# Loading the large expert's gate and up blocks by one transfer each instead of two

## The chip, the cores and the metric

The kernel runs on one core of a Trainium2 chip (8 cores, in two dies of four). The metric is device time in microseconds (us) of one launch, the median of several runs. The profile is one further execution, recorded by the hardware profiler. Five engines matter: TensorE (PE; PEld is its weight load), VectorE (DVE), ScalarE (ACT), GpSimd (POOL) and SyncE (SP), which here does nothing but wait and issue transfers. Every transfer is carried by the core's 16 DMA engines.

## What is computed

One decoder layer of 1024 tokens with 1024 columns: an mLSTM mixer, LayerNorm, then a mixture of 32 experts of which every token takes two, and a second LayerNorm. The change touches the experts alone:

```python
def expert_block(args):
    xblk, e = args
    hdn = jax.nn.silu(xblk @ w_gate[e]) * (xblk @ w_up[e])
    return hdn @ w_down[e]
```

The three matrices of an expert (gate 1024x512, up 1024x512, down 512x1024, float32) are 2 MB each, so the 32 experts are 192 MB of weights, and each weight is read once.

## The kernel before

The first 480 us or so hold the mixer, the first LayerNorm and the routing. Then come the experts, sorted by how many tokens they have and worked in sixteen pairs, n = 0 to 15: a large expert (up to 128 rows) and a small one (up to 64 rows). The last 50 us or so weight the experts' rows, add them up, normalise and store.

The large expert's matrices are multiplied in three passes of a faster number type: ACT copies a block into a high part (`hi_large`, line 1000, `whi`), DVE subtracts it to get the low part (`lo_large`, line 1739), and PE multiplies high by high, low by high and high by low (lines 1918 to 1920). Each of the blocks gate, up and down (k = 0, 1, 2) is 128 partitions of 16 KB, and it is handled in halves of 8 KB per partition (p = 0, 1): `halves(p)`. The buffers are single: `raw_b[0]` (named `raw` in the profile) takes the gate block, `raw_b[1]` the up block, `raw_b[2]` the down block. The low part overwrites the raw block in place, so a new block may only be loaded when PE is done with the old low part. The small expert's matrices are used in float32 as they are (lines 2342, 2343, 2360, 2361), from `raw_s`, `raw_up` and `raw_down`, also in halves.

Everything is ordered by hand-written program order on each engine and by semaphores. SP's list for pair i is: the small expert's gate and up halves p = 0 and then p = 1 (line 509, four transfers of 1 MB), the large down block (line 504, two transfers), the small down block (two), and then the next pair's large gate block (two) and large up block (two): twelve transfers of 1 MB. Each waits until PE has gone past the data that it overwrites: the gate halves wait on `g_mm`, which counts the halves of `gate_large`, the up halves on `u2_mm`. The semaphore `ex_landed[k][p]` tells ACT that a half has landed. SP issues the transfers of pairs 0 and 1 and of their blocks with fixed expert numbers; later ones take the number from the sorted list.

ACT's list for pair i (function `pair`) is, in order: the two down halves of `hi_large`; `silu_large`; `hidden_hi`; `hi_large(i + 1, 0, 0)`, the first gate half of the next pair; `silu_small` (line 1032); `xg_hi`; `hi_large(i + 1, 0, 1)`; `y_large`; `hidden_small`; the first up half; `y_large`; the second up half; `y_small`; `x_small`. ACT works this list strictly in order, so a half that hasn't landed holds up all behind it.

PE's list for pair i is: `gate_up_small(i, 0)`, `hidden_large(i)` (line 2311, needs the large silu by way of DVE's `gu_b`), `gate_up_small(i, 1)`, `rows_large(i + 1)` (line 2284), `down_large(i, 0)`, `hidden_small(i)` (line 2351, needs `silu_small` by way of DVE's `gu_s`), `down_large(i, 1)`, `down_small(i)`, `gate_large(i + 1)`, `rows_small(i + 1)` (line 2332), `up_large(i + 1)`. POOL gathers the tokens' rows for each expert and scatters the results to memory, on a queue of its own.

Of the kernel before, what the change touches and what calls it, by code (L numbers as in the profile page):

```python
# [44 lines left out]
FIRST = 2  # L45
# [26 lines left out]
def halves(p):  # L72

    return slice(p * HALF, (p + 1) * HALF)


def build(nc, x_rows, x_cols, meta_cols, w_in, b_gates, head_norm_w, w_out, ln1_g, ln1_b, w_group, b_group, w_router,
# [144 lines left out]
    def over(t, name, shape, dt=F32):  # L222
        return nc.alloc_sbuf_tensor_at(name, list(shape), dt, offset=offsets[t])
# [20 lines left out]
    raw_b = [raw[1], over("wlo1", "raw_b1", [P, PIECE]), over("wlo2", "raw_b2", [P, PIECE])]  # L244
# [109 lines left out]
    def sem(name):  # L354
        if name not in S:
            S[name] = nc.alloc_semaphore(name)
        return S[name]
# [3 lines left out]
    ex_landed = [[sem(f"ex_landed{k}_{p}") for p in range(2)] for k in range(3)]  # L361
# [25 lines left out]
    N = {n: sem(n) for n in names}  # L387

    gate_w = w_gate.rearrange("e (p k) n -> e p (k n)", k=KC)
    up_w = w_up.rearrange("e (p k) n -> e p (k n)", k=KC)  # L390
# [40 lines left out]
    def _(sp):  # L431
# [55 lines left out]
        def half_of(src, e, p):  # L487
            if isinstance(e, int):
                return src[e, :, halves(p)]
            return src[bass.ds(e, 1), :, halves(p)].rearrange("e p n -> p (e n)")  # L490
# [3 lines left out]
                sp.dma_start(raw_b[k][:, halves(p)], half_of((gate_w, up_w, down_w)[k], e, p)).then_inc(ex_landed[k][p], 16)  # L494

        def load_large(n, e, k):
            for p in range(2):
                if k == 0:
                    sp.wait_ge(N["g_mm"], n * 2 + (p - 1))
                elif k == 1:  # L500
                    sp.wait_ge(N["u2_mm"], n * 2 + (p - 1))
                else:
                    sp.wait_ge(N["y2_mm"], n * 3 + (p - 1))
                sp.dma_start(raw_b[k][:, halves(p)], half_of((gate_w, up_w, down_w)[k], e, p)).then_inc(ex_landed[k][p], 16)
# [57 lines left out]
        def load_next_large(i):  # L562
            if isinstance(i, int) and i + 1 < FIRST:
                large = i * 2 + 2
            else:
                if isinstance(i, int) and i + 1 == FIRST:
                    sp.wait_ge(N["ordered"], 1)
                large = expert_at(i * 2 + 2)
            load_large(i + 1, large, 0)
            load_large(i + 1, large, 1)  # L570

        def load_pair(i, ahead=1):
            fixed = isinstance(i, int) and i < FIRST
            small = i * 2 + 1 if fixed else expert_at(i * 2 + 1)
            for p in range(2):
                for k in range(2):
                    load_small(i, small, k, p)
            load_large(i, i * 2 if fixed else expert_at(i * 2), 2)
            for p in range(2):
                load_small(i, small, 2, p)  # L580
            if ahead:
                load_next_large(i)
# [245 lines left out]
    def _(act):  # L828
# [167 lines left out]
        def hi_large(n, k, p):  # L996
            if isinstance(n, int) and n == 0 and k == 2:
                act.wait_ge(N["y_mm"], 2 * NT)
            act.wait_ge(ex_landed[k][p], n * 16 + 16)
            a.activation(whi[k][:, halves(p)], raw_b[k][:, halves(p)], ACT.Copy).then_inc(e_hi[k], 1)  # L1000

        def xg_hi(n):
# [48 lines left out]
        for p in range(2):  # L1051
            hi_large(0, 0, p)
# [4 lines left out]
        act.wait_ge(N["h1_done"], NT + 1)  # L1057
        act.dma_start(h1_dram[T - P:T, :], z1[1][:]).then_inc(h1_stored[1], 16)
        hi_large(0, 1, 0)
        xg_hi(0)  # L1060
        hi_large(0, 1, 1)
        act.wait_ge(N["w_arg"], 1)
        a.activation(r_g4[:], r_g4[:], ACT.Exp)
# [1403 lines left out]
```

## Time and profile before

| | us |
|---|---|
| median of 3 runs | 1074.08 |
| lowest and highest | 1072.32, 1075.74 |
| the profiled execution | 1074.68 |
| its span | 1073.0 |

Busy shares of the span: PE 95%, PEld 68%, DVE 53%, ACT 40%, POOL 16%. The mean granted clock of PE is 0.987 of full speed. The program moves 288.17 MB in 71465 packets, 45812 of them under 8 KB. PE's busy time is modelled from pipelined matmuls and isn't a measure of how near it is to its peak. "DMA share" is the mean busy share of the 16 DMA engines; it can read slightly over 1 because a packet's bytes and time are booked at its end.

### The profile page before, as it was taken

The page shows a single profiled execution, that of the slowest core. Times are in us where ns is not written, and L with a number is a line of the kernel's source. Part 1 is how long each engine was busy: PE and PEld are TensorE (multiplying, and loading weights), DVE is VectorE, ACT ScalarE, POOL GpSimd, SP SyncE. Part 2 cuts the span into 40 slices and gives each one's busy share as a digit, 9 for nine tenths or more (in the row PEclk, how much of TensorE's full clock was granted, in tenths as well). Part 3 has the DMA queues.
Part 4 walks back from the last instruction along what each step waited for, and adds up shares of the span by engine and source line. Part 5 has one row for each costly group of instructions (what it writes and reads, how often), then busy time and mean ns, then how long its engine had stood idle before and what let it go on. Part 6 is the DMA issues. An engine that isn't in the chain of part 4 may idle for free.

```text
span 1073.0 us, 14469 instructions
## 1 busy us (share of the span) xinstructions
PE 1019.5 (95%) x5051; PEld 733.5 (68%) x5051; DVE 565.7 (53%) x1040; ACT 434.0 (40%) x574; POOL 173.7 (16%) x208
## 2 busy tenths in 40 slices
PE   8999999999999999999999989989998989989993
PEld 7878999778888788866665556646564556645541
DVE  4320503135465787878556645454445535465488
ACT  5322213223435410024555535454455535555452
POOL 3101111100000000012232212302332113430200
PEclk9999999999999999999999999989999999999997
DMA  8613314541211543456999999999999999999893
GB/s 301 242 47 121 123 44 133 172 146 40 80 42 60 196 157 138 177 203 220 400 418 414 413 412 404 383 386 403 415 401 374 415 402 387 419 385 406 349 359 157
DMA packets 71465, 288.17 MB, mean 269 GB/s; under 512 B 14352, under 2 KB 22680, under 8 KB 45812
## 3 DMA queue, kind: packets, MB, share of 16 engines
q1 hardware_dynamic: 60336, 258.35, 62.0%
q0 software_dynamic: 9920, 24.94, 6.1%
q10 hardware_dynamic: 1156, 4.20, 1.0%
q8 instruction: 32, 0.52, 0.2%
q14 instruction: 21, 0.17, 0.1%
HBM read 262.47 MB, written 33.56 MB: 276 GB/s over the span
## 4 chain that ended last, share of the span: by engine, by line
PE 66%; DMA 19%; DVE 6%; issue 4%; ACT 3%; DVEq 2%; POOL 0%; SPq 0%; POOLq 0%; ACTq 0%
PE bank L1918 15%; DMA raw_b<-l_w_down 14%; PE bank L1920 14%; PE bank L1919 14%; PE bank L2342 6%; DMA raw<-l_w_gate 5%; PE bank L2360 2%; ACT whi L1000 2%; PE bank L2103 1%; PE bank L2105 1%; PE bank L2284 1%; PE bank L2108 1%; PE bank L2152 1%; PE bank L2351 1%; PE bank L2311 1%
## 5 line engine op out<-in xcount | busy, mean ns | idle before, releaser
L1739 DVE TENSOR_TENSOR wlo<-raw_b,whi 128x2048 fp32r<-128x2048 f32 x64 | 146.0, 2289 | 171.8 <-ACT whi L1000 170.7
L1000 ACT ACTIVATE whi<-raw_b 128x2048 fp32r<-128x2048 f32 x64 | 122.1, 1912 | 47.8 <-DMA raw_b<-l_w_down 47.4
L2342 PE MATMUL bank<-raw_up,xT_s 128*64 128x512 f32 x256 | 123.7, 628 | 0.0
L2343 PE MATMUL bank<-raw_s,xT_s 128*64 128x512 f32 x256 | 123.7, 628 | 0.0
L1918 PE MATMUL bank<-whi,x_blocks 128*128 128x512 f32 x288 | 115.5, 401 | 0.9 <-ACT num L947 0.6
L1920 PE MATMUL bank<-whi,x_blocks 128*128 128x512 f32 x288 | 112.4, 390 | 0.0
L1919 PE MATMUL bank<-wlo,x_blocks 128*128 128x512 f32 x288 | 112.3, 390 | 0.0
L1918 PE MATMUL bank<-whi,xghi 128*128 128x512 f32 x256 | 103.4, 404 | 0.0
L1920 PE MATMUL bank<-whi,xglo 128*128 128x512 f32 x256 | 99.7, 389 | 0.0
L1739 DVE TENSOR_TENSOR lo_b<-raw,whi 128x2048 fp32r<-128x2048 f32 x32 | 73.2, 2287 | 42.8 <-ACT whi L1000 41.8
L2342 PEld LDWEIGHTS bank<-raw_up,xT_s 128*64 128x64 f32 x256 | 34.0, 143 | 67.9 <-issue 66.1
L1000 ACT ACTIVATE whi<-raw 128x2048 fp32r<-128x2048 f32 x32 | 61.1, 1913 | 24.1 <-DMA raw<-l_w_gate 19.5
L1918 PEld LDWEIGHTS bank<-whi,xghi 128*128 128x128 f32 x256 | 48.0, 188 | 22.7 <-issue 12.4
L1918 PEld LDWEIGHTS bank<-whi,x_blocks 128*128 128x128 f32 x288 | 54.1, 188 | 12.2 <-issue 1.8
L1920 PEld LDWEIGHTS bank<-whi,x_blocks 128*128 128x128 f32 x288 | 54.1, 188 | 11.7
L1919 PEld LDWEIGHTS bank<-wlo,x_blocks 128*128 128x128 f32 x288 | 54.2, 188 | 10.0
L1183 DVE TENSOR_TENSOR wlo<-raw,whi 128x2048 fp32r<-128x2048 f32 x10 | 22.5, 2288 | 69.5 <-ACT whi L834 69.5
L2360 PE MATMUL bank<-raw_down,hT_s 128*64 128x512 f32 x128 | 58.4, 598 | 0.0
L2361 PE MATMUL bank<-raw_down,hT_s 128*64 128x512 f32 x128 | 58.4, 598 | 0.0
L1920 PEld LDWEIGHTS bank<-whi,xglo 128*128 128x128 f32 x256 | 48.1, 188 | 10.4
L1918 PE MATMUL bank<-whi,ghi 128*128 128x512 f32 x128 | 53.6, 419 | 0.0
L1919 PE MATMUL bank<-wlo,ghi 128*128 128x512 f32 x128 | 50.1, 392 | 0.0
(425 smaller groups left out, 2017.7 us busy)
## 6 DMA issues: line engine op xcount, KB each, us to landing
raw<-l_w_gate SPq DMA_DIRECT2D x32, 1024.0 KB, 17.3
raw_b<-l_w_down SPq DMA_DIRECT2D x32, 1024.0 KB
raw_up<-l_w_up SPq DMA_DIRECT2D x32, 1024.0 KB
raw_down<-l_w_down SPq DMA_DIRECT2D x32, 1024.0 KB
raw_s<-l_w_gate SPq DMA_DIRECT2D x32, 1024.0 KB
raw_b<-l_w_up SPq DMA_DIRECT2D x32, 1024.0 KB, 15.8
raw<-l_w_in SPq DMA_DIRECT2D x5, 2048.0 KB, 9.5
yy<-expert_rows SPq DMA_DIRECT2D x8, 1024.0 KB, 8.6
```

Source lines behind the costliest of these rows:

```text
L1000: a.activation(whi[k][:, halves(p)], raw_b[k][:, halves(p)], ACT.Copy).then_inc(e_hi[k], 1)
L1183: tt(wlo[g % 2][:, c], raw[g % 2][:, c], whi[g % 2][:, c].bitcast(F32), ALU.subtract).then_inc(N["lo_done"], 1)
L1739: tt(lo_b[k][:, halves(p)], raw_b[k][:, halves(p)], whi[k][:, halves(p)].bitcast(F32), ALU.subtract).then_inc(e_lo[k], 1)
L1918: t.matmul(out, lh, rh, start=first, stop=False)
L1919: t.matmul(out, lh, rl, start=False, stop=False)
L1920: return t.matmul(out, ll, rh, start=False, stop=last)
L2103: t.matmul(ps[N_BANK[h % 2]][:, 0:DV + 1], ew[:, h, :], vext[c % 2][:, h, :], start=True, stop=False)
L2105: t.matmul(ps[N_BANK[h % 2]][:, 0:DV + 1], qsT[:, h, :], cst[:, h, :], start=False, stop=True).then_inc(N["n_mm"], 1)
L2342: t.matmul(ps[7][0:SMALL, :], xT_s[:, kk, :], wu[:, kk, :], start=kk == 0, stop=kk == KC - 1)
L2343: last = t.matmul(ps[7][SMALL:, :], xT_s[:, kk, :], wg[:, kk, :], start=kk == 0, stop=kk == KC - 1)
L2360: t.matmul(ps[7][0:SMALL, :], hT_s[:, k, :], wd[:, k, 0:512], start=k == 0, stop=k == FC - 1)
L2361: last = t.matmul(ps[7][SMALL:, :], hT_s[:, k, :], wd[:, k, 512:], start=k == 0, stop=k == FC - 1)
```

## The change

From n = 2 on, the gate block and the up block of the large expert are each loaded by one transfer of 128 rows of 16 KB. It waits until both halves of the old block have been used, and it signals `ex_landed[k][0]` alone. Both halves of `hi_large` wait for that one semaphore. The down block, all small blocks, and pairs 0 and 1 stay as they are.

```diff
         def load_large(n, e, k):
+            if k < 2 and not (isinstance(n, int) and n < FIRST):
+                sp.wait_ge((N["g_mm"], N["u2_mm"])[k], n * 2)
+                whole = (gate_w, up_w)[k]
+                sp.dma_start(raw_b[k][:], whole[e] if isinstance(e, int) else whole[bass.ds(e, 1)].rearrange("e p n -> p (e n)")).then_inc(ex_landed[k][0], 16)
+                return
             for p in range(2):
                 if k == 0:
                     sp.wait_ge(N["g_mm"], n * 2 + (p - 1))
@@
         def hi_large(n, k, p):
             if isinstance(n, int) and n == 0 and k == 2:
                 act.wait_ge(N["y_mm"], 2 * NT)
-            act.wait_ge(ex_landed[k][p], n * 16 + 16)
+            halves_land = k == 2 or (isinstance(n, int) and n < FIRST)
+            act.wait_ge(ex_landed[k][p if halves_land else 0], n * 16 + 16)
             a.activation(whi[k][:, halves(p)], raw_b[k][:, halves(p)], ACT.Copy).then_inc(e_hi[k], 1)
```

## Rows read from the trace of the kernel before

**Rows 1.** The page's 40 slices: DMA busy tenths, and what they moved.

```profile
DMA  8613314541211543456999999999999999999893
GB/s 301 242 47 121 123 44 133 172 146 40 80 42 60 196 157 138 177 203 220 400 418 414 413 412 404 383 386 403 415 401 374 415 402 387 419 385 406 349 359 157
```

**Rows 2.** Windows: busy us (instructions) by engine, PE clock, DMA share, GB/s.

```profile
571.00:595.00 24.00, 24.00 (x114) 15.94 (x111) 12.34 (x13) 13.32 (x14) 6.97 (x8) 1.00 1.01 425
605.00:1000.00 395.00, 368.66 (x1693) 226.32 (x1690) 198.55 (x138) 200.56 (x199) 102.09 (x92) 0.98 1.00 400
712.00:724.00 12.00, 12.00 (x58) 7.11 (x56) 8.80 (x6) 8.31 (x10) 1.83 (x4) 0.96 0.91 361
636.00:642.00 6.00, 5.50 (x20) 2.02 (x20) 2.99 (x4) 2.51 (x2) 0.00 (x0) 0.72 1.01 426
```

**Rows 3.** The chain that ended last, 580 to 1010: start, us, what.

```profile
587.84 17.26 DMA raw<-l_w_gate
605.13 1.92 ACT whi L1000
...
613.89 17.69 DMA raw_b<-l_w_down
...
991.91 15.29 DMA raw_b<-l_w_down
```

**Rows 4.** DMA packets of 12:20, 571:595 and 605:1000, and gate issues in 605:1000.

```profile
DMA packets 1369, 3.28 MB, mean 411 GB/s; under 512 B 49, under 2 KB 56, under 8 KB 1369
...
DMA packets 1606, 10.21 MB, mean 425 GB/s; under 512 B 219, under 2 KB 219, under 8 KB 503
...
DMA packets 25040, 157.87 MB, mean 400 GB/s; under 512 B 4332, under 2 KB 4332, under 8 KB 7222
...
raw<-l_w_gate SPq DMA_DIRECT2D x22, 1024.0 KB, 18.0
```

**Rows 5.** SP's timeline, gate and up issues in pairs 3 and 6.

```profile
620.43 3.05 SPq L504 DMA_DIRECT2D raw<-l_w_gate  x2
626.98 3.05 SPq L504 DMA_DIRECT2D raw_b<-l_w_up  x2
...
728.81 3.05 SPq L504 DMA_DIRECT2D raw<-l_w_gate  x2
```

**Rows 6.** Who waited for whom in the whole trace: us in total, times, longest.

```profile
ACT whi L1000 <- DMA raw_b<-l_w_down: 47.4, 26, 4.7
...
PE bank L2311 <- DVE gu_b L1761: 25.2, 12, 5.2
...
ACT whi L1000 <- DMA raw<-l_w_gate: 19.5, 13, 3.1
```

**Rows 7.** ACT's timeline in pairs 3 and 14: gate halves and small silu.

```profile
605.13 1.91 ACT L1000 ACTIVATE whi<-raw 128x2048 fp32r<-128x2048 f32 x1 [2.60 <-DMA raw<-l_w_gate]
607.06 0.60 ACT L1032 ACTIVATE sg_s<-bank 64x512 f32<-64x512 f32 x1
...
608.65 1.91 ACT L1000 ACTIVATE whi<-raw 128x2048 fp32r<-128x2048 f32 x1
...
984.59 0.60 ACT L1032 ACTIVATE sg_s<-bank 64x512 f32<-64x512 f32 x1
```

**Rows 8.** PE's timeline: small and large hidden transposes of pairs 3, 5 and 14 (the large ones of the pair after).

```profile
610.10 0.66 PE L2351 MATMUL bank<-ident,gu_s 64*128 64x64 f32 x4 [0.76 <-DVE gu_s L1770]
...
636.50 0.75 PE L2311 MATMUL bank<-ident,gu_b 128*128 128x128 f32 x4 [3.24 <-DVE gu_b L1761]
...
678.97 0.66 PE L2351 MATMUL bank<-ident,gu_s 64*128 64x64 f32 x4 [1.34 <-DVE gu_s L1770]
...
708.12 1.12 PE L2311 MATMUL bank<-ident,gu_b 128*128 128x128 f32 x4 [5.23 <-DVE gu_b L1761]
...
988.09 0.69 PE L2351 MATMUL bank<-ident,gu_s 64*128 64x64 f32 x4
...
1012.12 0.75 PE L2311 MATMUL bank<-ident,gu_b 128*128 128x128 f32 x4 [0.84 <-DVE gu_b L1761]
```

## The prediction

> **What bounds the kernel now.** I read the page's slices first. From about 510 us to 1000 us the DMA engines are busy nine tenths or more in every slice and move some 400 GB/s [rows 1]. That is the expert stage. The windows say it closer: a share of 1.00 to 1.01 throughout, 425 GB/s in a good stretch, 400 GB/s as the mean of 605:1000 [rows 2]. PE is busy 368.66 us of those 395, so it idles too, and the chain shows why: it runs through a gate load of 17.26 us and a down load of 17.69 us, each time followed by ACT's copy, and in between there is only PE work [rows 3]. A gate half takes 18.0 us from issue to landing [rows 4], although 1 MB (1.05e6 bytes) at 425 GB/s needs only 2.47 us. So some 15 us of other transfers stand before it in the queue. The stage is bound by how fast the queue drains; when a transfer is issued hardly matters as long as the queue stays filled. What the reader should keep in mind is where this bound touches the engines: ACT waits for landings, 47.4 us for down and 19.5 us for gate [rows 6], and since ACT works in order, PE then waits 25.2 us ahead of line 2311 for a silu that stood behind the down copies. These waits are the slack with which PE pays for being faster than the queue.
>
> **The change part by part.**
>
> *Packets.* Pairs 2 to 15 have two merged blocks each: 28 blocks, 28 transfers fewer. A half is 128 rows of 8 KB on 16 engines, that is 8 packets an engine, and one very small packet an engine tells that it has ended (the packets under 512 B). So each block saves 8 row packets and 1 end packet per engine, 28 x 9 = 252. The price of a packet comes from two full stretches. In 12:20 there are 1369 packets of 2.4 KB, 16 x 8 us / 1369 = 93.5 ns each; in 571:595 there are 1606 of 6.4 KB, 16 x 24 us / 1606 = 239.1 ns each [rows 4]. The straight line through both is 5.4 ns a packet and 0.0368 ns a byte (435 GB/s without packets). The saving is 252 x 5.4 ns = 1.4 us. No row shows a 16 KB packet, so the bounds are wide. At one end nothing is saved, if a row is cut into the old packets anyway. At the other end: by the same line the 157.87 MB and 25040 packets of 605:1000 should take (25040 x 5.4 ns + 157.87e6 x 0.0368 ns) / 16 = 371 us, and they take 395. These 24 us are slow packets and thin queues. Gate and up have 22 issues each there, 44 x 1.05 = 46 of the 157.87 MB, 29%; if long rows freed them of all of it, that would be 7 us more, 8.4 in all. I take 1.4: the line is drawn through measured stretches, and 571:595 is nearest in kind, 8 KB rows in a full queue; nothing in the rows ties the 24 us to the length of rows.
>
> The Trainium skill (DMA: Bandwidth & Descriptors, Anatomy of one DMA, and Bandwidth) gives a transfer about 2.0 us fixed and bytes/436e3 us, and wants transfers of 1 MiB and more. By it each merged block would save 2.0 us, 56 us for the 28, if transfers followed each other one by one; the rows of 571:595 show the opposite, 425 GB/s with 1 MB transfers, so that fixed part already lies beside others' data.
>
> *Issue.* The first half is no longer issued when half the old block is used but with the second. In SP's rows the two issues of a block span 3.05 us and the single one takes some 0.35, so the first goes out 2.7 us later [rows 5]. The second goes out when it did. Behind it on SP stand the up block, which waits for a later PE event anyway, and the next small blocks, which also do. With 15 us of queue ahead, 2.7 us are hidden. The cover is thinnest after a long stall: in 712:724 the share is 0.91 and the rate 361 GB/s [rows 2], and the gate issue comes at 728.81, right behind the pair's large and small down blocks, 4 transfers that alone take 9.9 us. If the cover were gone, each such place would cost up to 2.7 us. I take zero.
>
> *Landing.* Now the first gate half is seen only when the whole block has landed. That is later by the second half's transfer: at least 2.47 us, and under 3.5 us, as in pair 3 the second copy starts at 608.65 without a wait, 3.5 us after the first [rows 7]. ACT is waiting for exactly this half in 13 pairs (2 to 14), and behind it stands the small silu. In pair 3 the silu moves from 607.06 to 609.5. From the silu to the small transposes (line 2351) it is 3.04 us (607.06 to 610.10), and PE already stood 0.76 us there; so PE loses 2.5 us, likewise in pair 5 [rows 8]. In pair 14 the silu at 984.59 becomes 987.1, the transposes 990.1 instead of 988.09: 2.0 us. The same working for all thirteen pairs gives 0 to 2.5 us each and 20 us together. It is not added to the time, since the next thing PE waits for is the down block, which comes out of the queue when it did: PE idles 3.24 us at 636.50 and 5.23 us at 708.12 [rows 8], and such idle sums to 25.2 us over 12 pairs [rows 6]. A loss of 2.5 there is paid out of an idle of 2 to 5. The last pair is the exception: its idle is 0.84 us against a loss of 2.0, so 1.2 us come through: the last down block's landing ends the stage, and no later idle pays for them. The up block is harmless: its copies stand later in ACT's list, where second halves are taken without a wait, and PE uses them 10 us later.
>
> The Trainium skill (same page, Why a DMA increments its semaphore by 16 and not by 1) says that only the full count tells that data has landed, and an intermediate one not which bytes. That speaks against the change: ACT can't start on the first 8 KB of a row that is there. The rows agree in so far as ACT's copies begin only at landings.
>
> *ACT's second wait* on the same semaphore passes at once: nothing. *POOL's* gathers and scatters share the engines with longer packets and may land a few us later; they are asked for some 20 us ahead, so nothing.
>
> *Sum*, against the profiled 1074.68: -1.4 + 1.2 = -0.2, so 1074.5; against the median of 1074.08 it is 1073.9. The profiled execution is 0.6 above the median and inside the span of the three runs.
>
> **Rivals.**
>
> *Faster: long rows raise the rate.* The queue is the bound, so each per cent of rate counts in full. For it: 400 GB/s as the mean against 425 in a good stretch. Against it: 8 KB rows already reach 425 of the 435 that the line gives. Price between 1.4 and 8.4 us, middle 5: 1069. Chance 0.21.
>
> *Slower: the stall moves to line 2351 and takes the clock down.* Three pairs, of which 3 and 5 are shown, would have an idle of over 3.1 us there (0.76 + 2.5 in pair 3, 1.34 + 2.5 in pair 5) [rows 8]. After the idle of 3.24 us at 636.50 the granted clock was 0.72 over 636:642 [rows 2], between 1.2 and 2.4 GHz, so 6 x 0.28 = 1.7 us of work were lost. It decides from where loss and slow clock together (2.5 + 1.7) exceed the idle ahead of line 2311, which is about 3 us in most pairs; then the small blocks are released later and the queue gets as thin as in 712:724. Three such places with 1.7 us and 1.2 at the end make 6.3 us, with no gain from packets: 1080.4. Against it: the idle ahead of line 2311 shrinks by what is lost before, so there the clock stays up. Chance 0.21.
>
> *The change does nothing to packets*: rows are cut as before. Then only the 1.2 us are left: 1075.3. Chance 0.06. My forecast has 0.52.
>
> **How the numbers follow.** About 0.3%, 3.2 us, is what a measurement of this kernel can tell from no change. The forecast and the last rival lie within it: 0.58. Faster by more 0.21, slower by more 0.21. The range reaches into both outer cases, down to 1068.5 (just past the middle of the faster one) and up to 1079.5 (just short of the slower one's 1080.4), leaving out some 0.2.
>
> **What would show it.** Right: 252 x 16 = 4032 packets fewer; SP's gate issue as one, at the time of the old second; ACT's wait for gate longer by some 2.5 us in each of 13 pairs and PE's wait ahead of line 2351 up from near nothing to 15 to 20 us; PE's wait ahead of line 2311 down by about as much; the last down block landed some 1 us earlier than 1007.2 (991.91 + 15.29) [rows 3]. Wrong: a rate of 605:1000 clearly over 400 GB/s (the faster rival), or a share below 0.97 and more stretches of half clock (the slower one). The sum also fails if the down block lands later than it did, for then PE's idle is no cover.

## The result, and the profile after

| | before | changed |
|---|---|---|
| median of 22 runs each, us | 1073.97 | 1078.15 |
| lowest and highest | 1072.23, 1084.05 | 1075.30, 1084.08 |
| ratio, 95% interval | | 1.0035 (1.0022 to 1.0048) |
| span of the profiled execution | 1073.0 | 1077.6 |
| mean granted clock of PE | 0.987 | 0.978 |

The changed kernel is slower by some 4 us, where no change was forecast (1073.9 us, within the 0.3% that a measurement can tell). The line numbers move: 1000 becomes 1006, 1032 becomes 1038, 2311 becomes 2317, 2351 becomes 2357.

4032 packets fewer for the same bytes, and a rate over the stage that isn't higher. First the page's line of packets, then the stage as a window (busy us of each engine, granted clock, DMA share, GB/s), then its packets:

```profile
DMA packets 67433, 288.17 MB, mean 267 GB/s; under 512 B 13904, under 2 KB 22232, under 8 KB 45364
```

```profile
605.00:1000.00 395.00, 373.20 (x1696) 230.56 (x1694) 196.71 (x144) 197.40 (x198) 92.60 (x91) 0.97 1.00 399
```

```profile
DMA packets 21633, 157.75 MB, mean 399 GB/s; under 512 B 3946, under 2 KB 3946, under 8 KB 6816
```

Against [rows 2, 4] that is 399 GB/s beside 400, with a share of 1.00 in both. Then who waited for whom (total us, times, longest), to be laid beside [rows 6]:

```profile
ACT whi L1006 <- DMA raw<-l_w_gate: 48.8, 14, 5.2
...
PE bank L2357 <- DVE gu_s L1776: 24.6, 13, 3.5
...
ACT whi L1006 <- DMA raw_b<-l_w_down: 5.5, 8, 0.9
...
PE bank L2317 <- DVE gu_b L1767: 0.5, 1, 0.5
```

Ahead of the small transposes PE had waited for this in the kernel before:

```profile
PE bank L2351 <- DVE gu_s L1770: 2.8, 3, 1.3
```

ACT's wait has changed places: from down (47.4 us, now 5.5) to gate (19.5, now 48.8). PE's wait went with it: 25.2 us ahead of the large hidden transposes have become 0.5, and 2.8 us ahead of the small ones have become 24.6. In sum nothing was added (28.0 us before, 25.1 now). The queue stays full as before, and PE just stands in another place.

The end of the stage differs. First the chain of waits (start, us, what), then ACT's and PE's timeline of pairs 14 and 15:

```profile
974.83 13.75 DMA raw<-l_w_gate
...
992.75 0.68 DVE gu_s L1776
```

```profile
988.60 1.91 ACT L1006 ACTIVATE whi<-raw 128x2048 fp32r<-128x2048 f32 x1 [2.27 <-DMA raw<-l_w_gate]
...
1008.01 3.71 ACT L1006 ACTIVATE whi<-raw_b 128x2048 fp32r<-128x2048 f32 x2
```

```profile
993.57 0.66 PE L2357 MATMUL bank<-ident,gu_s 64*128 64x64 f32 x4 [0.52 <-DVE gu_s L1776]
...
1016.66 0.75 PE L2317 MATMUL bank<-ident,gu_b 128*128 128x128 f32 x4
```

The first gate copy of pair 15 in the kernel before was this:

```profile
982.65 1.91 ACT L1000 ACTIVATE whi<-raw 128x2048 fp32r<-128x2048 f32 x1 [1.23 <-DMA raw<-l_w_gate]
```

Before, the last DMA step in the chain was the last down block [rows 3], and PE stood 0.84 us for it at 1012.12 [rows 8]. Now it is the last gate block, n = 15. Its landing at 988.60 starts ACT's copy, and from there the chain goes through ACT, DVE and PE with no further transfer. Both down copies run back to back at 1008.01 without a wait, and PE comes to its transposes at 1016.66 without one. The profiled execution of the changed kernel was already 1.9 us late before the first merged transfer (its large transposes of pair 0 start at 508.76, before 506.88). Of the 4.5 us at the last large transposes (1016.66 - 1012.12) 2.6 us are therefore the stage's, and the tail behind adds nothing.

One thing in these two profiles doesn't come from the last landing. PE's large transposes of pair 14 stand ahead of it, and they are late already (before, then changed):

```profile
979.96 0.75 PE L2311 MATMUL bank<-ident,gu_b 128*128 128x128 f32 x4 [2.15 <-DVE gu_b L1761]
```

```profile
984.86 0.75 PE L2317 MATMUL bank<-ident,gu_b 128*128 128x128 f32 x4
```

That is 4.9 us, 3.0 without the late start. SP issues the last gate block late, too, since the issue waits for PE: at 974.83, where the second half went out at 967.7 before (the pair of issues starts at 964.98, the second some 2.7 us on). Less the 1.9 us of late start this is 5.2 us.

```profile
964.98 3.05 SPq L504 DMA_DIRECT2D raw<-l_w_gate  x2
```

### The profile page after: what moved, and what is told of

Its sections match the earlier page's. It is cut to its first block, busy times and chain, and to the rows that moved or that the text cites. A ratio compares the mean times of both kernels' runs of the same rounds, so it can differ in the third digit from the quotient of the medians.

```text
span 1077.6 us, 14399 instructions
## 1 busy us (share of the span) xinstructions
PE 1027.1 (95%) x5051; PEld 741.4 (69%) x5051; DVE 564.0 (52%) x1040; ACT 430.8 (40%) x574; POOL 171.6 (16%) x208
## 4 chain that ended last, share of the span: by engine, by line
PE 66%; DMA 19%; DVE 6%; issue 4%; ACT 3%; DVEq 2%; SPq 0%; ACTq 0%
DMA raw<-l_w_gate 18%; PE bank L1924 16%; PE bank L1926 15%; PE bank L1925 15%; PE bank L2366 5%; ACT whi L1006 2%; PE bank L2348 2%; PE bank L2109 1%; PE bank L2111 1%; PE bank L2114 1%; PE bank L2357 1%; PE bank L2158 1%; DVE gu_s L1776 1%; PE bank L2427 1%; PE bank L2431 1%
## 5 line engine op out<-in xcount | busy, mean ns | idle before, releaser
L2348 PE MATMUL bank<-raw_up,xT_s 128*64 128x512 f32 x256 | 116.7, 599 | 0.0
L2349 PE MATMUL bank<-raw_s,xT_s 128*64 128x512 f32 x256 | 116.7, 598 | 0.0
L1006 ACT ACTIVATE whi<-raw 128x2048 fp32r<-128x2048 f32 x32 | 61.1, 1913 | 53.4 <-DMA raw<-l_w_gate 48.8
L1924 PE MATMUL bank<-whi,ghi 128*128 128x512 f32 x128 | 59.0, 461 | 0.0
L1925 PE MATMUL bank<-wlo,ghi 128*128 128x512 f32 x128 | 55.3, 432 | 0.0
```

Source lines behind the costliest of these rows:

```text
L1924: t.matmul(out, lh, rh, start=first, stop=False)
L1925: t.matmul(out, lh, rl, start=False, stop=False)
L2348: t.matmul(ps[7][0:SMALL, :], xT_s[:, kk, :], wu[:, kk, :], start=kk == 0, stop=kk == KC - 1)
L2349: last = t.matmul(ps[7][SMALL:, :], xT_s[:, kk, :], wg[:, kk, :], start=kk == 0, stop=kk == KC - 1)
```

## The experiments

All times are against the kernel before on the same chip; 0.3% is 3.2 us. "Held" says that ACT's first gate copy waits for the whole block ahead of the small silu.

| kernel | gate transfer | held | ratio (95%) |
|---|---|---|---|
| changed | merged | all pairs | 1.0035 (1.0022 to 1.0048) |
| changed, again | merged | all pairs | 1.0043 (1.0022 to 1.0065) |
| only gate merged | merged | all pairs | 1.0046 (1.0030 to 1.0061) |
| only up merged | halves | no | 1.0007 (0.9992 to 1.0021) |
| late issue | halves | no | 0.9995 (0.9981 to 1.0010) |
| late look | halves | all pairs | 1.0018 (1.0004 to 1.0032) |
| both late | halves | all pairs | 1.0027 (1.0007 to 1.0047) |
| both late, gate only | halves | all pairs | 1.0013 (0.9991 to 1.0035) |
| changed, small silu first | merged | no | 1.0013 (0.9987 to 1.0038) |
| the same, again | merged | no | 0.9990 (0.9968 to 1.0012) |
| before, small silu first | halves | no | 0.9999 (0.9979 to 1.0019) |
| changed, PE kept busy | merged | all pairs | 1.0044 (1.0021 to 1.0067) |
| changed but the last gate | merged, last in halves | all but the last | 1.0022 (1.0004 to 1.0040) |
| only the last gate merged | halves, last merged | last | 1.0041 (1.0020 to 1.0062) |
| last pair written out (control) | halves | no | 0.9987 (0.9966 to 1.0008) |
| the control, last pair held | halves | last | 1.0021 (0.9996 to 1.0047) |
| first three merged | merged for n = 2, 3, 4 | those | 1.0001 (0.9981 to 1.0021) |

### Issue, look or transfer

The change does three things: it issues the first half later, it looks at it later, and it makes rows of 16 KB. Each could be the cause, and the expectations name them by letters. Theory A is the late look: ACT holds the small silu until the whole gate block is there. Theory B is the late issue of the first half. Theory C is that rows of 16 KB are slow in the queue. The first runs take one each. Late issue (in `load_large`):

```diff
-                    sp.wait_ge(N["g_mm"], n * 2 + (p - 1))
+                    sp.wait_ge(N["g_mm"], n * 2 + (0 if late else p - 1))
```

(the same for `u2_mm`; `late` is true from n = 2 on)

> From the third pair on, the first halves of gate and up are issued only when PE has used both halves of the old block, 2.7 us later than before; rows stay 8 KB and ACT looks at each half by itself. Theory A expects nothing, within 1 us of before, as some 15 us of queue stand ahead of the transfer. Theory B expects the loss here: +3 to +4 us. Theory C expects nothing.

Ratio 0.9995: the late issue by itself costs nothing that can be measured (at most 1 us by its interval). Theory B falls as a cause by itself.

Late look (in `hi_large`):

```diff
+            if k < 2 and p == 0 and not (isinstance(n, int) and n < FIRST):
+                act.wait_ge(ex_landed[k][1], n * 16 + 16)
             act.wait_ge(ex_landed[k][p], n * 16 + 16)
```

> From the third pair on, gate and up stay two transfers of 8 KB rows, issued when they always were, but ACT's first copy of each block waits for both halves. Theory A (the late look: ACT, which works in order, holds the small silu until the whole gate block is there, and PE stands at the small hidden transposes) expects most of the change's loss: +3 to +4 us against before, the waiting of PE moved from the large to the small hidden transposes. Theory B (the late issue of the first half) expects no loss, within 1 us of before. Theory C (16 KB rows are slow in the queue) expects no loss either.

Ratio 1.0018, +1.9 us. Its waits have the changed kernel's pattern without any merged transfer:

```profile
ACT whi L1002 <- DMA raw<-l_w_gate: 47.3, 14, 5.3
...
PE bank L2353 <- DVE gu_s L1772: 24.1, 13, 3.5
...
ACT whi L1002 <- DMA raw_b<-l_w_down: 7.1, 11, 1.2
```

So the moved waits are the late look's doing, as theory A says, but only about half of the loss came with them (0.4 to 3.4 us by the interval).

One block each:

```diff
-            if k < 2 and not (isinstance(n, int) and n < FIRST):
+            if k == 0 and not (isinstance(n, int) and n < FIRST):
```

(`k == 1` for up, and `halves_land` to match)

> Only the gate block is merged into one transfer of 16 KB rows, up stays in halves. Theory A expects the whole loss, +3 to +5 us, since only the gate copy stands ahead of the small silu. Theory C expects half of the loss, +2 us. Theory B expects at least half, too.

> Only the up block is merged into one transfer of 16 KB rows, gate stays in halves. Theory A expects no loss, and if fewer packets are worth something a gain of up to 0.7 us (half of the forecast 1.4): -0.7 to 0. Theory C expects the other half of the loss, +2 us. Theory B expects +2 us.

1.0046 and 1.0007: the loss is in gate, and none is seen in up (its interval ends at +2.3 us). Half of the long rows are thus free of loss, and free of gain too. Both late edits together, for both blocks and for gate alone, keep 8 KB rows and give the rest of the change:

> Everything of the change but the merged transfer: from the third pair on the two gate halves and the two up halves go out together, at the time of the second, as 8 KB rows, and ACT looks only when both are there. The late look alone gave a ratio of 1.0018, the gate merged alone 1.0046. If the rest of the loss is in the 16 KB rows (theory C), this gives +1.5 to +2.5 us against before, like the late look alone. If late issue and late look add up to more than each alone (theory A with B), it gives the change's whole +4.

> Only gate, as two transfers of 8 KB rows that go out together at the time of the second, and ACT looks when both are there: the counterpart of the run with only gate merged (1.0046). If the merged transfer itself costs (16 KB rows land later than two transfers of 8 KB rows), this gives +1.5 to +3 us against before; if not, +4 to +5.

1.0027 and 1.0013. The three held kernels with halves give +1.4 to +2.9 us, the three merged ones +3.8 to +4.9. The changed kernel, repeated beside the first of them:

> The changed kernel once more, on the chip of its neighbours: +3 to +5 us against before by every theory. Its trace should again have its waits at gate (45 to 50 us) and a last gate landing 4 us later than that of the first half before.

### Taking the silu out from behind the gate copy

```diff
         def pair(i):
             ...
-            hi_large(i + 1, 0, 0)
             silu_small(i)
             xg_hi(i + 1)
+            hi_large(i + 1, 0, 0)
             hi_large(i + 1, 0, 1)
```

(this is ACT's list; and on DVE `lo_large(i + 1, 0, 0)` behind `times_up_small(i)` and `xg_lo(i + 1)`)

> The changed kernel, but ACT does the small silu and the rows' high part before the first gate copy, and DVE the small product and the rows' low part before the first gate subtraction. Theory A (a copy that waits for the gate block holds up the small silu) expects the wait of PE at the small hidden transposes to vanish and the loss with it: within 1 us of before or faster. If the loss is in the queue (theory C), some +2 us stay.

> The changed kernel with the small silu ahead of the first gate copy, a second time (1.0013 with a wide interval the first time). If the held-up silu is the whole cause: within 1 us of before, both results together at 1.000 to 1.001. If the merged transfers cost by themselves: +2 us.

> The kernel before with the same reordering of ACT and DVE. Theory A expects it near before, 0 to -1 us: PE's waits at the small transposes sum to only 2.8 us there, and its wait for the down block stays. If it is faster by more, the order was costing more than its visible waits.

With the merged transfers as they are, 1.0013 and 0.9990: taken together the loss is gone, and no gain is seen. The first of them alone has an interval up to 4.1 us and would not show it. On its chip its median is 1075.96 us, against 1079.49 for the changed kernel. The kernel before doesn't care (0.9999). The waits of the first (PE at the large transposes for `gu_b`, ACT at down) are back where they were:

```profile
ACT whi L1006 <- DMA raw_b<-l_w_down: 48.0, 25, 4.0
...
PE bank L2317 <- DVE gu_b L1767: 25.7, 11, 4.4
```

So theory C falls as a cause by itself: the same packets cost nothing that is seen here once ACT no longer holds the silu for them.

### The clock

In the changed kernel the longest idle at the small transposes is 3.49 us (PE's timeline), and a window behind it has a granted clock of 0.50, the 1.2 GHz level:

```profile
651.42 0.71 PE L2357 MATMUL bank<-ident,gu_s 64*128 64x64 f32 x4 [3.49 <-DVE gu_s L1776]
```

```profile
651.00:657.00 6.00, 5.58 (x16) 4.35 (x16) 6.00 (x6) 3.44 (x4) 0.00 (x0) 0.50 0.97 385
```

The mean clock of the run is 0.978. Eight small matmuls ahead of the wait keep PE at work:

```diff
-        def hidden_small(s):
+        def hidden_small(s, ends=False):
+            if not ends and not (isinstance(s, int) and s < 2):
+                awake(4, 8)
             pe.wait_ge(N["gu_s_done"], s + 1)
```

(`ends` is true for the last pair alone.)

> The changed kernel, but from the third pair to the last but one PE does eight small matmuls on a constant (some 1.1 us at full clock, their result is overwritten) ahead of its wait for the small hidden product, in time that it idles. Theory F (part of the loss is the granted clock, which falls to the lower level after an idle at the small hidden transposes) expects the clock of the run back at 0.983 or more and 1 to 3 us of the loss gone, so +1 to +3 us against before. Without F it stays at +3.5 to +4.5, or is worse by what the matmuls cost.

The clock came back, to 1.00 over the stage, and the time did not:

```profile
605.00:1000.00 395.00, 382.78 (x1879) 246.44 (x1878) 197.78 (x140) 198.90 (x199) 84.37 (x91) 1.00 1.00 399
```

Ratio 1.0044, with an interval from 2.3 to 7.2 us: nothing of the loss is seen to come back. The falling clock accompanies the loss and isn't its main cause; a share of up to some 1.5 us (3.8 - 2.3) isn't excluded. While the queue sets the period, PE's speed is free. Behind the last gate block it isn't: in "both late, gate only" the granted clock was 0.58 over 990:993 and 0.85 over 993:996, behind the small transposes of pair 14, and there the end came 90.9 us after the start of the last gate copy, 2.0 us more than in the other kernels that hold it (below).

### One-off or pair by pair

If the queue absorbs the stall in every pair but the last (theory D), merging in the last pair alone must cost as much as in all, and merging in the first ones nothing. If the loss builds up pair by pair (theory E), one merged pair must cost next to nothing. For the first the pass i = last - 1 of SP's and ACT's pair loops is written out behind the loop:

```diff
-        with sp.Fori(4, last_pair) as i:
+        with sp.Fori(4, last_pair - 1) as i:
             load_pair(i)
+        load_pair(last_pair - 1, last=True)
```

and `last` picks whole or halves for the gate block n = 15.

> The kernel before, but the last pair's gate block alone is loaded by one transfer of 16 KB rows and seen as a whole. Theory D expects +1.5 to +2.5 us against before, theory E 0 to +0.5.

> The changed kernel, but the last pair's gate block (n = 15) is loaded and looked at in halves again; all else as changed. Theory D (the queue bounds all pairs but the last, and the loss is the last gate block's late landing, from which PE works through to the end) expects -2.5 us against the change, that is +1 to +2 us against before. Theory E (the loss builds up pair by pair, as every pair now runs from the gate landing) expects it to stay at +3.5 to +4.5.

1.0041 with one merged transfer in the whole kernel (seven runs), the size of the entire loss; theory E expected at most +0.5 us, and the interval starts at 2.1. And 1.0022 with all the others merged and this one not: about half of it back, at the upper end of the expected +1 to +2 us or a little above, with an interval that reaches from 0.4 to 4.3 us. The two don't add up to the changed kernel's loss (4.4 + 2.4 us against 3.8), but their intervals are wide enough for it. The control, the last pair held without any merged transfer, and the other end of the loop:

> Control: the kernel before, with the last but one pass of SP's and ACT's pair loops written out behind the loop. It computes and moves the same. If writing it out costs nothing: within 1 us of before, and the run with only the last gate merged (1.0041) and the one with all but the last merged (1.0022) stand as read. If it costs 2 us or more, both are to be read against this.

> The control, but in the last pair ACT's first gate copy waits for both 8 KB halves; nothing else. Theory D (one-off at the last pair) expects +1.5 to +2.5 us against the control; theory E (builds up) expects 0 to +0.3.

> Gate and up merged as in the change, but only for the third to the fifth pair (n = 2, 3, 4). Theory D expects nothing, within 1 us of before, since eleven pairs bound by the queue follow. Theory E expects 3 of 14 parts of the loss, +0.9 us, and the part of it from PE's first stalls, where the queue is still short, perhaps +1 to +2.

Writing the pair out costs nothing (0.9987). Holding the last pair alone gives 1.0021 (0.9996 to 1.0047), 2.6 us by the medians over the control (1076.29 against 1073.70). Three merged pairs at the start give 1.0001; that run can't tell the theories apart, as the +0.9 us of theory E lies inside its interval of 2 us either way. By the single merged transfer theory D holds for the greater part, and theory E falls as the whole account. That a part of the changed kernel's loss arises ahead of the last pair isn't excluded: the 1.0022 without the last merged transfer is above 1, and in the profiles PE was 3.0 us late at the large transposes of pair 14.

How the last landing sets the end is plain in ACT's timelines: the start of the last pair's first gate copy, in the changed kernel again, only gate merged, late look, and the control with the last pair held, one fence each.

```profile
990.06 1.92 ACT L1006 ACTIVATE whi<-raw 128x2048 fp32r<-128x2048 f32 x1 [3.41 <-DMA raw<-l_w_gate]
```

```profile
989.37 1.91 ACT L1006 ACTIVATE whi<-raw 128x2048 fp32r<-128x2048 f32 x1 [2.72 <-DMA raw<-l_w_gate]
```

```profile
982.57 1.91 ACT L1002 ACTIVATE whi<-raw 128x2048 fp32r<-128x2048 f32 x1 [2.25 <-DMA raw<-l_w_gate]
```

```profile
985.32 1.92 ACT L1003 ACTIVATE whi<-raw 128x2048 fp32r<-128x2048 f32 x1 [3.58 <-DMA raw<-l_w_gate]
```

Their spans are 1079.0, 1078.3, 1071.5 and 1074.3 us. Each is 88.9 to 89.0 us more than the start of that copy, and so is the changed kernel's (1077.6 - 988.60 = 89.0). It is 88.9 to 89.0 us in "both late", "changed, PE kept busy" and "only the last gate merged", too; the one exception is the 90.9 us of "both late, gate only" with its slow clock. When the last gate block is held, the end thus follows its landing and what PE does behind it. In the kernel before, that distance is 1073.0 - 982.65 = 90.35 us and in the control 1075.2 - 983.75 = 91.4: there something later, the down block, set the end, and the first half had some 1.4 us or more to spare.

## Why the prediction was wrong

*What bounds the kernel*: right, and it stayed so. 399 GB/s at a share of 1.00 after against 400 before.

*Issue*: right for the edit by itself, costed at nothing, measured 0.9995. But "the second goes out when it did" didn't hold in the last pair of the changed kernel: the block was issued 5.2 us later than the second half before, because PE was late. Whether that made it land later, or the queue ahead covered it, no run shows.

*Landing, pairs 2 to 13*: right. 20 us of PE's time were to go into waits at the small transposes and come out of those at the large ones; measured 21.8 us in (2.8 to 24.6) and 24.7 us out (25.2 to 0.5). For the three merged pairs at the start no cost is seen.

*Landing, the last pair*: this is the step that failed. It was the right place for the greater part of the loss, but its term was sized at 1.2 us: the whole block 2.47 us behind the first half, which costs PE 2.0 us at the small transposes, less the idle of 0.84. In the profiles the copy began at 988.60 against 982.65, less the 1.9 us of late start 4.05 us. Of that 1.4 us were slack (90.35 - 88.95), and 2.65 us came through. The slack was foreseen nearly right (2.47 - 1.2 = 1.3 us); the gap was not. The prediction's range for the gap went to 3.5 us, read off pair 3, but only the lower end went into the sum. And the timed runs ask for more than the profile: 4.2 us by the medians.

*Packets*: the gain of 1.4 us was counted in full against the end. That was sound as a sum, since the last gate block comes out of the same queue and would have landed earlier by it. But no run shows the gain: 1.0007 with up merged, 1.0013 and 0.9990 with both merged and the silu first. With intervals of 1.5 to 2.7 us either way these can't exclude 1.4 us, but they don't show it. The straight line through two stretches gave a price for packets of 2 to 6 KB; for 16 KB it wasn't confirmed. The fixed 2.0 us a transfer, which the Trainium skill (DMA: Bandwidth & Descriptors, Anatomy of one DMA) fits for transfers issued by way of GpSimd, was rightly left out of the sum for these transfers of SP: of the 56 us that it would give for 28 transfers fewer, no run shows any.

So -1.4 + 1.2 should have read 0 + 2.6, by the profile, or 0 + 4 by the runs: two errors of the same sign in a sum whose terms almost cancelled. The chance of 0.58 for no change rested on the last-pair term: at 1.2 us it lay within the 3.2 us even without any gain, at 4 us it doesn't.

*The slower rival*: its first half happened (an idle of 3.49 us, clock down to 0.50), its second didn't: kept at full clock the kernel is as slow. It had the sign, and 6.3 us against the measured 4, by another mechanism. *The faster rival* and *no change to packets* fell: the packets went down by 4032, as computed, and the rate stood.

What stays open: whether and why a merged last gate block is later than two halves looked at together. The timed runs say that it costs more: +4 us against +2, most clearly on one chip with medians of 1080.18 (only gate merged) and 1076.22 us (late look). In single profiles the last gate copy starts 475.0 to 478.2 us behind the large transposes of pair 0 in four held kernels with halves, and 479.8 to 482.4 us in the four with the change or gate merged throughout. (The kernel with only the last gate merged has 475.3 in its profiled execution, which was its fastest run, and says nothing on it.) But such a gap lies within what single executions differ by: the kernel with only the first three merged, whose last block came in halves, has 482.6 in its profiled execution, its slowest run. The late issue of the edit isn't it, as the both-late kernels have it too. Yet in the four merged ones SP issued the block later still, 464.6 to 467.4 us behind those transposes, against 461.3 to 463.3 for the second half in the four with halves. So the lateness was there before the transfer was issued, and the loop may have handed it on from pair to pair. Nor is it a lower rate of long rows as such, as the same transfers cost nothing with the silu first. None of the runs singles it out.

## What to carry to other kernels

When a queue sets the period of a loop, added stalls inside it can be free (22 us of new waits in 13 pairs here were paid out of old ones), and so can gains outside the queue. Then the loop's last pass must be costed by itself: follow the chain backwards from its end, take for each transfer in it the time to the end, and see which one is nearest to deciding. Here that was 89.0 us from the last gate block against 90.35 us available. The size of the delay must be bounded from above, too, not only taken at the time that the added bytes need: 2.47 us were taken and 4.05 us measured. A transfer shouldn't be made longer where an in-order engine waits for its first part ahead of other work; if it has to be, move the other work ahead of the wait, after which no loss was measured here (1.0013 and 0.9990).

## What the runs showed of the hardware

Rows of 16 KB were no faster than rows of 8 KB in a full queue: 396 to 399 GB/s over 605:1000 in the four kernels with the gate block merged and held throughout (changed, again, only gate merged, kept busy), 400 in the kernel before, 402 and 403 in late look and late issue, and 401 to 404 in up alone merged and the two with the silu first. Executions of kernels that differ by little are as far apart (397 with the first three merged, 401 in the control with the last pair held).

PE's granted clock was no measure of the kernel's speed: 1.00 over the stage in a kernel 4 us slower than the one with 0.98. And the single execution in a profile can mislead by as much as the effect: the kernel with only the last gate merged was profiled at 1073.29 us, with a median of 1078.88.
